# Query blocks of a retention layer by seven products, five products of the first token tile at the front, and the last gate product by column halves

## The reference, cut to what matters

```python
hn = rms_norm(h, mix_norm_g[i])
z = hn @ od_w_in[j]                       # 1024 -> 6144
q, k, v, g = _split(z, OD_SPLIT)          # 1024, 1024, 2048, 2048
yc = retention_mixer(q, k, v, g, od_gn_g[j])   # rotary on q and k first
h = h + yc @ od_w_out[j]
h = h + hier_moe(rms_norm(h, ffn_norm_g[i]), ...)   # 32 experts, each 3 weights of 2 MB
e = rms_norm(p[i] @ ple_w_up[i], ple_norm_g[i])
h = h + e * jax.nn.sigmoid(h @ ple_w_gate[i])       # the gate stage
```

## Time and profile before

| | |
|---|---|
| median of 3 runs | 1305.06 us (1304.95 to 1306.23) |
| the profiled execution | 1305.21 us, its span 1303.4 us |
| PE busy | 1042.9 us, 80% of the span |
| DVE, ACT, POOL busy | 483.2, 176.1, 108.6 us |
| mean granted clock of PE | 0.912 of full speed |
| HBM read | 472.08 MB, 365 GB/s over the span |

### The profile page before, as it was taken

How to read it: one execution, slowest core, us unless ns; L and a number is a source line. 1 busy time by engine, 2 the same in 40 slices (tenths; PEclk the granted TensorE clock), 3 DMA queues, 4 the chain that set the end, 5 groups by cost and what they waited for, 6 DMA issues and landing times.

```text
span 1303.4 us, 26625 instructions
## 1 busy us (share of the span) xinstructions
PE 1042.9 (80%) x11057; PEld 642.4 (49%) x11057; DVE 483.2 (37%) x965; ACT 176.1 (14%) x413; POOL 108.6 (8%) x233
## 2 busy tenths in 40 slices
PE   9999989667656666679999999989766667656778
PEld 7885545334333333344688884555433333333343
DVE  2987533111111111135784888524111111111117
ACT  2343201000000000012111110211000000000011
POOL 0010111000100001000110110011001000100000
PEclk9999989888888888899999999998888888888889
DMA  9876999999999999999444237899999999999992
GB/s 360 298 278 268 388 428 426 428 428 428 428 428 428 428 428 428 428 410 376 149 176 173 100 128 318 334 428 425 428 427 430 429 427 428 429 429 428 428 418 96
DMA packets 59266, 473.87 MB, mean 364 GB/s; under 512 B 4328, under 2 KB 6632, under 8 KB 34000
## 3 DMA queue, kind: packets, MB, share of 16 engines
q1 hardware_dynamic: 57952, 469.73, 87.3%
q10 hardware_dynamic: 912, 2.12, 0.4%
q0 software_dynamic: 352, 1.32, 0.3%
HBM read 472.08 MB, written 3.16 MB: 365 GB/s over the span
## 4 chain that ended last, share of the span: by engine, by line
PE 47%; DMA 45%; issue 3%; DVE 2%; SPq 1%; ACT 0%; POOL 0%; DVEq 0%; POOLq 0%; ACTq 0%
DMA big<-in_moe_w_up_dram 43%; PE ps L1054 10%; PE ps L772 6%; PE ps L1273 6%; PE ps L1293 4%; PE ps L1185 3%; PE ps L848 3%; PE ps L747 3%; DMA big<-in_moe_w_down_dram 2%; PE ps L1079 2%; PE ps L728 2%; PE ps L1087 1%; PE ps L738 1%; PE ps L1020 1%; PE ps L826 1%
## 5 line engine op out<-in xcount | busy, mean ns | idle before, releaser
L1054 PE MATMUL ps<-big 128*32 128x256 f32 x4048 | 322.7, 485 | 237.9 <-DMA big<-in_moe_w_up_dram 233.9
L1054 PEld LDWEIGHTS ps<-big 128*32 128x32 f32 x4048 | 167.5, 138 | 391.8 <-issue 230.6
L2003 DVE SCALAR_TENSOR_TENSOR wroute<-wroute,ps 64x256 f32<-64x256 f32 x64 | 26.4, 413 | 649.3 <-ACT wroute L1527 649.3
L1079 PE MATMUL ps<-big,r 128*32 128x256 f32 x2048 | 122.6, 379 | 2.2 <-DVE r L2012 2.1
L1527 ACT ACTIVATE wroute<-ps 64x256 f32<-64x256 f32 x64 | 24.2, 378 | 549.6 <-PE ps L1054 549.6
L2515 POOL TENSOR_TENSOR big<-big,rk 128x64 f32<-128x64 f32 x64 | 28.6, 447 | 727.0 <-PE ps L1066 707.9
L1079 PEld LDWEIGHTS ps<-big,r 128*32 128x32 f32 x2048 | 64.5, 110 | 37.3 <-DVE r L2012 3.8
L1087 PE MATMUL ps<-big 32*128 32x256 f32 x1024 | 73.3, 400 | 1.3 <-ACT big L1538 1.3
L1020 PE MATMUL ps<-xn,big 128*32 128x256 f32 x1024 | 67.3, 380 | 1.3 <-POOL big L2509 1.3
L1087 PEld LDWEIGHTS ps<-big 32*128 32x128 f32 x1024 | 46.3, 184 | 29.1 <-issue 27.7
L1377 ACT ACTIVATE big<-ps 128x256 f32<-128x256 f32 (+3 forms) x58 | 25.5, 454 | 173.7 <-PE ps L1273 48.5
(11 more groups left out here) (296 smaller groups left out, 1200.8 us busy)
## 6 DMA issues: line engine op xcount, KB each, us to landing
big<-in_moe_w_gate_dram SPq DMA_DIRECT2D x62, 2048.0 KB, 32.7
big<-in_moe_w_down_dram SPq DMA_DIRECT2D x61, 2048.0 KB, 38.5
big<-in_moe_w_up_dram SPq DMA_DIRECT2D x60, 2048.0 KB, 37.1
big<-in_od_w_in_dram SPq DMA_DIRECT2D x12, 2048.0 KB, 14.1
big<-in_ev_w_in_dram SPq DMA_DIRECT2D x5, 2048.0 KB, 21.3
big<-in_ple_w_gate_dram SPq DMA_DIRECT2D x8, 1024.0 KB, 19.6
big<-in_od_w_out_dram SPq DMA_DIRECT2D x4, 2048.0 KB, 7.9
big<-in_ev_w_out_dram SPq DMA_DIRECT2D x2, 2048.0 KB, 13.8
```

The costliest lines, as they stand in the source:

```text
L1054: ins = nc.tensor.matmul(ps[TOK * i:TOK * i + TOK, 5, 0:2 * P].rearrange("p (b n) -> p b n", b=2), xe[:, k, :], here, start=k == 0, stop=k ...
L1079: ins = nc.tensor.matmul(ps[TOK * q:TOK * q + TOK, 7, 0:QD], hidT[:, k, :], wd[:, k, q * QD:(q + 1) * QD], start=k == 0, stop=k == KF - 1)
```

## The change

1. `rq0` and `rq1` join `SEVEN`: their direct products and rotations from PSUM go, and they take the path of the keys (seven products, sums on DVE, rotation from SBUF). Their buffers move (`kept_at`, `raws`).
2. PE begins the projection with `FIRST_TILE`: products a of `rq0`, a of `rq1`, a2 of `rq0`, a2 of `rq1`, then the transposes of the second token tile, then a of `rk0`. All five need the first token tile alone. Then the remaining products follow block by block, and the transposes of a rotated block come after the products of the block behind it.
3. DVE makes the third and the first tile of `rq0` inside `next_rows(1)`, around `normalise`; `token_sums` makes S3 first and has the second and fourth tile of `rq0` in between. ACT copies the first products out before and after the norm of the second tile.
4. In layer 1's gate stage the products a and a2 are made in two column halves of 256, each with a bank of its own; tanh, the two DVE steps and the store of the last block follow by halves. ACT instead of DVE copies the transposes `hT1_10`.

The diff's core, in this order: the lists, SP's last store, PE's gate product and projection, ACT's last tanh and front, DVE's last steps, front and rotations.

```diff
+SEVEN = ("rq0", "rq1", "rk0", "rk1", "rv0", "rv1", "rv2", "rv3")
+FIRST_TILE = (0, "a"), (1, "a"), (0, "a2"), (1, "a2"), (2, "a")
...
-            RELEASE[f"rq{c}"], RELEASE[f"rk{c}"] = f"rq{c}_1", f"rk{c}_c2"
+            RELEASE[f"rq{c}"], RELEASE[f"rk{c}"] = f"rq{c}_c2", f"rk{c}_c2"
...
+                if n == 3:
+                    sync.wait_ge(half_ready, n + 1)
+                    sync.dma_start(out[0, t * P:(t + 1) * P, 0:QD], h[:, t, 0:QD]).then_inc(stored, 16)
+                    cols = slice(QD, BLK)
...
+                    def gate_product_by_halves(i, ks=range(HALF)):
+                        lhs, rhs = operands[i]
+                        for side, cols in (("", slice(0, QD)), ("r", slice(QD, BLK))):
...
+                                ins = nc.tensor.matmul(b[:, 0:QD], lhs[:, k, :], rhs[:, k, cols], start=k == 0 and i != "a2",
+                                                       stop=k == HALF - 1, skip_group_check=True)
...
-            for t in range(NT):
-                for c in range(2):
-                    taken(pe, f"mixT1_{t}{c}")
-                tokens([f"rq0_{t}"], slot(arrived("rq0"), KD, BLK), t)
-                tokens([f"rq1_{t}"], slot(arrived("rq1"), KD, BLK), t, range(HALF))
-                if t == 0:
-                    first_rows(1)
-                tokens([f"rq1_{t}"], slot("rq1", KD, BLK), t, range(HALF, KD))
...
+                    if m == 0 and i in sums:
+                        pe.wait_ge(sums_ready, sums[i])
...
-            turn_rotated(0)
-            pe.wait_ge(sums_ready, 4)
+            for c in range(2):
+                taken(pe, f"mixT1_0{c}")
+            for m, i in FIRST_TILE[:-1]:
+                products(m, (i,))
+            first_rows(1)
+            for m, i in FIRST_TILE[-1:]:
+                products(m, (i,))
+            for c in range(2):
+                taken(pe, f"mixT1_1{c}")
             for m in range(len(SEVEN)):
-                products(m)
-                if m < 3:
-                    turn_rotated(m + 1)
+                products(m, [i for i in PRODUCTS if (m, i) not in FIRST_TILE])
+                if 1 <= m <= 4:
+                    turn_rotated(m - 1)
...
+                        if l:
+                            full(act, "gate1_a2r")
+                            emptied("gate1_a2r", sc.activation(own[:, QD:BLK], bank("gate1_a2r")[:, 0:QD], ACT.Tanh, scale=0.5))
...
+            for m, i in FIRST_TILE[:2]:
+                product_out(m, i)
+            norm(2, lambda t: (h_ready, NT * 2 + t + 1), (1,))
+            for m, i in FIRST_TILE[2:-1]:
+                product_out(m, i)
+            mixed(1)
+            for m, i in FIRST_TILE[-1:]:
+                product_out(m, i)
...
-                    gated(3)
+                    gated(3, 0)
+                    gated(3, 1)
...
                     dve.sem_inc(h_ready, 1)
+                    if t:
+                        third_tile(0)
                     normalise(2, t)
+                    if t:
+                        first_tile(0)
...
-                ve.tensor_tensor(S1, A21, A22, ALU.add).then_inc(sums_ready, 1)
                 ve.tensor_tensor(S3, A11, A21, ALU.subtract).then_inc(sums_ready, 1)
+                taken(dve, "mixT1_11")
+                ve.tensor_tensor(S1, A21, A22, ALU.add).then_inc(sums_ready, 1)
                 dve.wait_ge(sums_ready, 2)
+                second_tile(0)
                 ve.tensor_tensor(S2, S1, A11, ALU.subtract).then_inc(sums_ready, 1)
+                fourth_tile(0)
...
             dve.wait_ge(odd_loaded, 32)
             def rotate(n, source, done):
...
-            for c in range(2):
-                for t in range(NT):
-                    name = f"rq{c}_{t}"
-                    full(dve, name)
-                    rotate(2 * c + t, bank(name), lambda ins: emptied(name, ins))
...
-                if c == 0:
-                    token_sums()
-                    for make in (third_tile, first_tile, second_tile, fourth_tile):
-                        make(0)
+            taken(dve, "mixT1_00")
+            taken(dve, "mixT1_10")
+            token_sums()
...
-                if m < 2:
+                if m < 4:
                     for i in ("a2", "b2", "c2"):
                         taken(dve, f"{w}_{i}")
                     dve.wait_ge(values_ready, m + 1)
                     for t in range(NT):
-                        rotate(4 + 2 * m + t, rkraw[:, t, :], v)
+                        rotate(2 * m + t, product_of(m, t), v)
```

More of the change, by code:

```diff
@@ L118 @@
 RG_STEPS = ("a", "b", "d"), ("c", "a2", "b2", "c2")
-SEVEN = ("rk0", "rk1", "rv0", "rv1", "rv2", "rv3")
+SEVEN = ("rq0", "rq1", "rk0", "rk1", "rv0", "rv1", "rv2", "rv3")
+FIRST_TILE = (0, "a"), (1, "a"), (0, "a2"), (1, "a2"), (2, "a")
 LAST_BANKS = {"rout_01": "yT3_0", "rout_10": "yT3_1"}
@@ L141, in pe_jobs @@
                      [f"acc{l}_{q}" for q in SEED_ORDER] + [f"up{l}_00", f"up{l}_10", f"count{l}"])
-    after = lambda l: ([f"hT{l}_00", f"hT{l}_01", f"gate{l}_a", f"hT{l}_10", f"hT{l}_11"] +
-                       [f"gate{l}_{i}" for i in GATE_ORDER[l][1:]])
+    after = lambda l: ([f"hT{l}_00", f"hT{l}_01", f"gate{l}_a"] + ["gate1_ar"] * l + [f"hT{l}_10", f"hT{l}_11"] +
+                       [f"gate{l}_{i}" for i in GATE_ORDER[l][1:]] + ["gate1_a2r"] * l)
     first_tile = ["mixT1_00", "mixT1_01"]
@@ L151, in pe_jobs @@
     jobs += moe(0) + after(0) + first_tile
-    jobs += ["rq0_0", "rq1_0", "mixT1_10", "mixT1_11", "rq0_1", "rq1_1"]
-    jobs += [f"rq0T_{t}" for t in range(NT)]
+    jobs += [f"{SEVEN[m]}_{i}" for m, i in FIRST_TILE[:-1]] + ["mixT1_10", "mixT1_11"]
+    jobs += [f"{SEVEN[m]}_{i}" for m, i in FIRST_TILE[-1:]]
     for m, w in enumerate(SEVEN):
-        jobs += [f"{w}_{i}" for i in PRODUCTS] + ([f"{ROTATED[m + 1]}T_{t}" for t in range(NT)] if m < 3 else [])
+        jobs += [f"{w}_{i}" for i in PRODUCTS if (m, i) not in FIRST_TILE]
+        jobs += [f"{ROTATED[m - 1]}T_{t}" for t in range(NT)] if 1 <= m <= 4 else []
     jobs += ["rg0_a", "rg0_b"]
@@ L182, in banks_of @@
         fixed |= {f"mixT0_{i}{j}": 2 * i + j for i in range(2) for j in range(2)} | {f"iq{i}": 4 + i for i in range(4)}
-        fixed |= {"rstd": 0, "ikw": 1, "bias": 3, "gain0": 3, "rq0_0": 0, "rq1_0": 1, "rq0_1": 2, "rq1_1": 3}
+        fixed |= {"rstd": 0, "ikw": 1, "bias": 3, "gain0": 3}
         fixed |= {f"rg{c}_{i}": 4 + "abdc".index(i[0]) for c in range(4) for i in PRODUCTS}
@@ L188, in banks_of @@
         fixed |= {f"hT{l}_00": 4, f"hT{l}_01": 5, f"hT{l}_10": 7, f"hT{l}_11": 4}
+        fixed |= {"gate1_ar": 5, "gate1_a2r": 5}
         fixed |= {f"gate{l}_{i}": b for i, b in (("a", 6), ("a2", 6), ("b", 7), ("d", 0), ("b2", 1), ("c", 2), ("c2", 3))}
@@ L327, in trunk @@
         T2, T3, T4 = (view(ro_start + 1024 * i, HALF, VD) for i in range(3))
-        kept_products = [[view((5120 + BLK if m == 1 else 4096 if m % 2 else ro_start + 3072) + VD * i, VD) for i in range(4)]
-                         for m in range(len(SEVEN))]
-        rkraw = view(5120 + NH * VD + BLK, NT, 512)
+        kept_at = 15872, 0, ro_start + 3072, 5120 + BLK, ro_start + 3072, 4096, ro_start + 3072, 4096
+        kept_products = [[view(o1 + VD * i, VD) for i in range(4)] for o1 in kept_at]
+        kept_products[1] = [view(o1, VD) for o1 in (5120, 5376, 8704, 8960)]
+        raws = [view(o1, NT, 512) for o1 in (7680, 6656)]
         def out_quarters(l, pair):
@@ L503, in trunk @@
         for c in range(2):
-            RELEASE[f"rq{c}"], RELEASE[f"rk{c}"] = f"rq{c}_1", f"rk{c}_c2"
+            RELEASE[f"rq{c}"], RELEASE[f"rk{c}"] = f"rq{c}_c2", f"rk{c}_c2"
         def product_of(m, t):
-            return rkraw[:, t, :] if m < 2 else rv[:, t, (m - 2) * 512:(m - 1) * 512]
+            return raws[m % 2][:, t, :] if m < 4 else rv[:, t, (m - 4) * 512:(m - 3) * 512]
         def quarters(m):
@@ L698, in _ @@
                 cols = slice(half * BLK, (half + 1) * BLK)
-                sync.wait_ge(half_ready, n + 1)
+                if n == 3:
+                    sync.wait_ge(half_ready, n + 1)
+                    sync.dma_start(out[0, t * P:(t + 1) * P, 0:QD], h[:, t, 0:QD]).then_inc(stored, 16)
+                    cols = slice(QD, BLK)
+                sync.wait_ge(half_ready, n + 1 + (n == 3))
                 sync.dma_start(out[0, t * P:(t + 1) * P, cols], h[:, t, cols]).then_inc(stored, 16)
-            sync.wait_ge(stored, 32 * NT)
+            sync.wait_ge(stored, 16 * (2 * NT + 1))
         @block.tensor
@@ L1188, in gate_product @@
                             end(name, ins)
+                    def gate_product_by_halves(i, ks=range(HALF)):
+                        lhs, rhs = operands[i]
+                        for side, cols in (("", slice(0, QD)), ("r", slice(QD, BLK))):
+                            name = f"gate1_{i}{side}"
+                            b = bank(name) if ks[0] else begin(name)
+                            for k in ks:
+                                if k % 2 == 0:
```

(84 more changed lines are left out.)

2 lines of the change are left out of this document (removed).

## The result

The changed kernel takes 1307.89 us in the median of 16 runs (1306.41 to 1310.1), the kernel before 1305.6 in 16 runs beside it (1303.94 to 1306.99): ratio 1.0021, 95% interval 1.0014 to 1.0028. It is slower, by about as much as can be told from no change. The profiled execution took 1310.1 us, the longest of the 16 (span 1308.3 against 1303.4); of the two more profiles further down one is of an execution near the median (1307.58), the other of one near the top (1309.73).

The account below looks back on a forecast made before the run. In the projection the prediction took time to be PE's work plus any wait PE meets. Its terms, -3.28 + 5.0 + 1.9 - 0.8 = +2.8 us on 1305.21, gave 1308.0 us, range 1304.9 to 1309.7.

Parts of the forecast that it names:

- Products: Projection on PE: two query blocks by seven products instead of directly, 3.28 us less.
- The front on PE and ACT: Second tile's transposes, due after four products: its rows are scaled in time by 0.2 us, so PE doesn't wait.
- The wait: Projection's front: product c of `rq0` needs S3, behind DVE's wait for `c_rope`; PE stands 5.0 us.
- The bounds, 1.5 to 2.5 us: Gate blocks begin 1.7 us later, net; 1.5 if the landing doesn't move, 2.5 if POOL's issue slips 1.2 us.
- The clock: PE behind the stall at the front: granted clock falls to 0.50, costing 1.9 us, from 1.25 to 2.84.
- DVE behind the front: First blocks of the projection: DVE keeps up with PE by a margin of 1 to 3 us, cost 0.
- The end: Last gate product by halves: 0.8 us less behind PE's end; the smaller store may give 0.1.
- The sum: Whole kernel: +2.8 us on the profiled execution's 1305.21 us, giving 1308.0.
- An early landing of the constants: Rival at the front: `c_rope` lands before about 617.3, stall 0.6 us, clock stays; 1301.7 us, chance 0.10.
- The stall without the clock's part: Rival at the front: PE stalls but its clock stays; +0.9 us, 1306.1, chance 0.12.
- DVE falling behind: Rival behind the front: DVE's margin is used up, another 1 to 2 us, 1309.5; chance 0.10.

Follow-up runs that it names:

- the wait moved: Changed kernel with DVE's wait for the two constants moved from ahead of the token sums to behind them: 1301.06 us, ratio 0.9964 to the kernel before.
- The run with four products: Kernel with the wait moved, but four first-tile products at the front, not five; a of `rk0` back in its block: 1303.04 us, ratio 0.9981.
- the second profile: Another profiled execution of the changed kernel, unaltered: 1307.58 us.
- the third profile: A further profiled execution of the changed kernel, unaltered: 1309.73 us.
- the first profile: The profiled execution of the changed kernel, unaltered, among its 16 runs: 1310.1 us.
- the second experiment: Changed kernel with POOL issuing the two constants ahead of the second tile's root, DVE's wait where it was: 1303.39 us, ratio 0.9978.
- the third: As an experiment: changed kernel with 20 unused matmuls on PE ahead of product c of `rq0`: 1305.92 us, ratio 1.0004.

## Why the prediction was right

**Products.** -3.28 us was predicted; with the wait moved the projection is 104.36 - 101.10 = 3.26 us shorter.

**The front on PE and ACT.** The transposes of the second tile begin without a wait, as predicted (margin 0.2 us). The run with four products shows how thin that cover is: without 1.73 us of it PE waits 1.39, so the margin was about 0.3.

**The wait.** The place and the releaser are those predicted: S3 behind `c_rope`. The size, 5.0 us, lies between the executions' 3.62, 4.78 and 5.94. The bounds, 1.5 to 2.5 us net of the saving, were too narrow: net of 3.28 us the three are 0.34, 1.50 and 2.66. By its own terms the upper bound is 1.5 + 1.2 = 2.7. The prediction moved the landing along with everything ahead of it, and the profiles show that the two don't move together. In the second profile PE ends its fifth product at 617.88 and in the third at 616.80, but `c_rope` lands at 620.54 and 620.61: the shorter wait is PE's later arrival. Between the third and the first it is the landing that differs (621.64). What sets the landing stays open. The end of the projection was to be 3 to 4 us later than 711.41; it was 5.9, 3.6 and 4.7.

**The clock.** 1.9 us was taken, the mean of the groups in the experts' stage; 1.92, 2.94 and 3.12 were measured, or 1.69, 2.71 and 2.89 without the 0.23 us of the wait itself; the upper bound was 2.84. To read the rows as a step, free up to 3.93 us and slow from 4.02, was wrong: a wait of 3.62 us cost 1.92 here. The kernel before had such a row already, 5.35 us and not 3.66 for the same group after a wait of only 2.87:

```profile
1260.09 5.35 PE L1054 MATMUL ps<-big 128*32 128x256 f32 x64 [2.87 <-DMA big<-in_moe_w_up_dram]
```

**DVE behind the front.** It never held PE. In the three profiles the slow clock gave it time; with the wait moved and PE at full clock the margin was thinnest, 0.5 us (the third tile of `rk0` is made at 634.17, its product begins at 634.68), and still no PE wait appears in the chain.

**The end.** -0.8 us: 0.76 to DVE's last step, and 0.3 more behind it, where 0.1 was thought possible.

**The sum.** +2.8 us on the profiled execution, +2.3 measured between the medians. The mechanism was right; that 1308.0 came within 0.1 us of the median, 1307.89, is luck in part. The executions spread over 3.7 us, and the sum started from 1305.21, which is 0.4 under the median of the 16 runs of the kernel before. In the first profile wait and clock cost 9.1 us, the products 3.3, the end 1.1: +4.7, and the spans are 4.9 apart. For the median, 2.3 + 3.3 + 1.1 = 6.7 us of wait and clock are needed; that is worked back and not measured, and lies between the second and the third profile.

**The rivals.** An early landing of the constants, the rival on the other side, is what the second experiment makes in part by hand, with a stall of 1.52 us and not 0.6, and it then gives 0.9978, 1303.39 us and not 1301.7. The stall without the clock's part is the third, 1305.92 against 1306.1 predicted. DVE falling behind didn't occur.

The kernel with the wait moved takes less time than both, 1301.06 us: it has what the change was made of, 3.3 us in the products and 1.1 at the end, without the wait.

## What to carry to other kernels

When work is moved ahead in one engine's program, look at what stands in front of it in the programs of the engines that feed it: a wait that cost nothing in its old place holds all that is put behind it. Place a wait at the first instruction that reads the data, not at the head of a stage. And price a stall on PE with the time behind it: here the slow clock added about half of the wait again.

## What the runs showed of the hardware

- A 256 KB load from POOL's queue stood behind a queue of weights; the DMA engines' busy share fell under a half between 618.5 and 619.5 us. In the eight profiles in which it was issued between 613.6 and 615.0 us it took 5.5 to 7.9 us and landed between 620.1 and 621.6, and the later issues didn't land later. Issued at 609.06, it took 9.1 us: 4.7 us sooner than in the changed kernel's profile brought 3.5.
- The 80 records behind a PE wait of 3.62 us took 1.92 us more than 17.27, those behind one of 5.94 took 3.12 more, both with a granted clock of 0.50 in a part of them; behind one of 1.52 us it was 0.23, at 1.00. In the experts' stage of the kernel before, a wait of 3.93 us cost nothing and one of 2.87 cost 1.69 (5.35 against 3.66). With unused matmuls in the wait the clock stayed at 1.00. So the length of a wait alone doesn't tell its price.
